# Sixth slab of filler products moved from the softmax heads to the recurrent heads, in both mixings of a two-block model

## The reference, cut to what matters

```python
def token_mixing(x, norm_g, w_in, ..., w_out):
    h = rmsnorm(x, norm_g)
    proj = h @ w_in            # pool, ml q k v o i f, fox q k v f, and 3 x 1024 gate columns
    ...
    y_pool = pool_mixer(u_pool, pool_w_grp, pool_scale) @ w_br_pool
    y_ml = mlstm_mixer(ml_q, ml_k, ml_v, ml_o, ml_i + ml_b_i, ml_f + ml_b_f, ml_norm_g) @ w_br_ml
    y_fox = fox_mixer(fx_q, fx_k, fx_v, fx_f + fox_b_f) @ w_br_fox
    gts = jax.nn.sigmoid(gate_pre).reshape(gate_pre.shape[:-1] + (N_BRANCH, D_MODEL))
    merged = gts[..., 0, :] * y_pool + gts[..., 1, :] * y_ml + gts[..., 2, :] * y_fox
    return merged @ w_out
```

## Time and profile before

| what | value |
|---|---|
| median of 3 runs | 2291.81 us (2286.31 to 2295.19) |
| profiled execution, its own time | 2291.82 us |
| its span, first to last instruction | 2290.1 us |
| TensorE matmul busy | 2216.6 us, 97% |
| TensorE weight load busy | 1579.4 us, 69% |
| VectorE busy | 883.7 us, 39% |
| ScalarE busy | 393.3 us, 17% |
| mean granted TensorE clock | 0.985 |

### The profile page before, as it was taken

How to read it: one execution, slowest core, us unless ns; L and a number is a source line. 1 busy time by engine, 2 the same in 40 slices (tenths; PEclk the granted TensorE clock), 3 DMA queues, 4 the chain that set the end, 5 groups by cost and what they waited for, 6 DMA issues and landing times. The chain is left out here.

```text
span 2290.1 us, 49032 instructions
## 1 busy us (share of the span) xinstructions
PE 2216.6 (97%) x22096; PEld 1579.4 (69%) x22096; DVE 883.7 (39%) x1657; ACT 393.3 (17%) x822; POOL 169.4 (7%) x250
## 2 busy tenths in 40 slices
PE   8999999999999999999999999999998999899998
PEld 7699889998689973535353534344446877689997
DVE  2676455452566431010000100111013374768764
ACT  0242311100233320000000010000001342224302
POOL 1000100000000012000000000000001162400000
PEclk9999999999999999999999999999999997899999
DMA  7423354434333377999999999999997211055440
GB/s 248 148 93 130 122 210 158 162 129 166 111 108 123 102 276 281 403 387 393 416 411 417 413 411 414 409 415 408 415 404 261 94 38 39 10 189 187 148 182 20
DMA packets 170559, 540.96 MB, mean 236 GB/s; under 512 B 17068, under 2 KB 35022, under 8 KB 153966
## 3 DMA queue, kind: packets, MB, share of 16 engines
q1 hardware_dynamic: 154144, 528.81, 60.0%
q10 hardware_dynamic: 14622, 4.16, 0.8%
q0 software_dynamic: 1584, 4.85, 0.5%
HBM read 532.94 MB, written 4.85 MB: 235 GB/s over the span
## 5 line engine op out<-in xcount | busy, mean ns | idle before, releaser
L183 PE MATMUL bank<-ring,moe_he 128*32 128x512 f32 (+2 forms) x6144 | 577.7, 537 | 2.8 <-DMA ring<-in_moe_w_up 2.7
L183 PEld LDWEIGHTS bank<-ring,moe_he 128*32 128x32 f32 x6144 | 198.7, 110 | 376.6 <-issue 367.7
L183 PE MATMUL bank<-hT,ring 128*128 128x128 f32 (+1 forms) x1952 | 290.7, 307 | 9.7 <-PEq L932 3.4
L183 PE MATMUL bank<-ring,moe_actT 128*32 128x256 f32 x5352 | 292.3, 379 | 1.3 <-DMA ring<-in_moe_w_down 1.3
L183 PEld LDWEIGHTS bank<-hT,ring 128*128 128x128 f32 x1952 | 263.4, 191 | 33.4 <-issue 8.8
L183 PEld LDWEIGHTS bank<-ring,moe_actT 128*32 128x32 f32 x5352 | 174.1, 110 | 116.9 <-issue 3.9
L2784 DVE TENSOR_TENSOR moe_act<-moe_silu,bank 128x512 f32<-128x512 f32 (+2 forms) x48 | 26.8, 614 | 540.4 <-PE bank L183 540.4
L183 PE MATMUL bank<-ring 128*128 128x128 f32 (+2 forms) x976 | 121.8, 284 | 1.4 <-ACT ring L826 1.4
L183 PEld LDWEIGHTS bank<-ring 128*128 128x128 f32 (+1 forms) x976 | 115.8, 190 | 4.0 <-ACT ring L826 1.8
L183 PE MATMUL bank<-kept,ring 128*128 128x256 f32 (+1 forms) x448 | 96.6, 378 | 6.1 <-PEq L1709 3.0
L183 PEld LDWEIGHTS bank<-kept,ring 128*128 128x128 f32 x448 | 83.2, 198 | 18.5 <-issue 5.4
(11 more groups left out here) (841 smaller groups left out, 2553.1 us busy)
## 6 DMA issues: line engine op xcount, KB each, us to landing
ring<-in_moe_w_down SPq DMA_DIRECT2D x55, 2048.0 KB, 19.1
ring<-in_moe_w_gate SPq DMA_DIRECT2D x32, 2048.0 KB, 23.2
ring<-in_moe_w_up SPq DMA_DIRECT2D x32, 2048.0 KB, 22.8
ring<-in_w_in SPq DMA_DIRECT2D x29, 2048.0 KB, 8.0
ring<-in_moe_w_gate SPq DMA_DIRECT2D x28, 1536.0 KB, 18.1
ring<-in_moe_w_up SPq DMA_DIRECT2D x28, 1536.0 KB, 14.6
ring<-in_w_up SPq DMA_DIRECT2D x10, 2048.0 KB, 11.9
ring<-in_w_out SPq DMA_DIRECT2D x6, 2048.0 KB, 7.9
```

The costliest lines, as they stand in the source:

```text
L183: ins = pe.matmul(out, lhsT, rhs, start=start, stop=stop, **kw)
```

## The change

The unit list of the recurrent block gets a sixth slab (42 units in place of 35), the list of the softmax block loses it (30 in place of 37). The counts are set anew, and VectorE's sums and additions stand at other places of its stream.

```diff
-MIX_LATER = 5
-MLSTM_SHARES = (2,) * 16 + (3,)
+MIX_LATER = 6
+MLSTM_SHARES = (2, 3) + (3, 2, 3, 2) * 3 + (2, 2, 3)
 FOX_LEAD = 2
 FOX_FIRST = (3,) * 8
-FOX_SECOND = (2, 2, 2, 1, 1, 1, 1, 1)
+FOX_SECOND = (1, 1, 0, 1, 0, 1, 0, 0)
@@ fox_units
-    return branch(0) + seven(5) + branch(1) + seven(6) + branch(2) + seven(7) + branch(3)
+    return branch(0) + seven(6) + branch(1) + seven(7) + branch(2) + branch(3)
@@ mlstm, VectorE, head i
                 divide(i)
                 if 2 <= i + 1 < ML_HEADS:
                     weigh(i + 1)
-                if i < 2:
-                    fill.add_00(v, k, i)
+                if i == 0:
+                    fill.add_00(v, k, 0)
                 elif i == 2:
-                    fill.add_rest(v, k, 2)
-                else:
-                    fill.add_rest(v, k, 3)
-                    fill.sum_weights(v, k, 4)
-                norm(i)
-                if i < 2:
-                    fill.add_rest(v, k, i)
-                    fill.sum_weights(v, k, i + 1)
-                    exponents(i + 2)
-                if i == 1:
-                    fill.add_00(v, k, 2)
-                elif i == 2:
-                    fill.sum_weights(v, k, 3)
                     fill.add_00(v, k, 3)
                 elif i == 3:
                     fill.add_00(v, k, 4)
                     fill.add_rest(v, k, 4)
+                    fill.sum_weights(v, k, 5)
+                norm(i)
+                if i == 0:
+                    fill.add_rest(v, k, 0)
+                if i < 2:
+                    fill.sum_weights(v, k, i + 1)
+                    if i == 1:
+                        fill.add_00(v, k, 2)
+                    exponents(i + 2)
+                if i == 0:
+                    fill.add_00(v, k, 1)
+                    fill.add_rest(v, k, 1)
+                elif i == 1:
+                    fill.add_rest(v, k, 2)
+                    fill.sum_weights(v, k, 3)
+                elif i == 2:
+                    fill.add_rest(v, k, 3)
+                    fill.sum_weights(v, k, 4)
+                elif i == 3:
+                    fill.add_00(v, k, 5)
+                    fill.add_rest(v, k, 5)
@@ attention, VectorE, behind the copy of head i's transposes
-                    if i in (0, 2, 4):
-                        if i == 4:
-                            fill.add_rest(v, k, 6)
-                        fill.sum_weights(v, k, 5 + i // 2)
-                    elif i in (1, 3, 5):
-                        fill.add_00(v, k, 5 + i // 2)
-                    if i in (1, 6):
-                        fill.add_rest(v, k, 5 if i == 1 else 7)
+                    if i == 0:
+                        fill.sum_weights(v, k, 6)
+                    elif i in (1, 4):
+                        fill.add_00(v, k, 6 if i == 1 else 7)
+                    elif i in (2, 5):
+                        fill.add_rest(v, k, 6 if i == 2 else 7)
+                        if i == 2:
+                            fill.sum_weights(v, k, 7)
```

## The result

The changed kernel takes 2327.44 us in the median of 4 runs (2325.86 to 2328.39), the kernel before 2292.21 beside it: ratio 1.0151, 95% interval 1.0138 to 1.0165. It is 35.2 us slower. The forecast was 28 us slower, at 2320 with a range to 2331. The profiled execution has a span of 2325.9 us, 35.8 more than before.

The account below looks back on a forecast made before the run. TensorE was taken to bound both blocks. Per mixing 12.5 + 9.9 - 2.95 - 7.0 + 1.7 = 14.1 us, for two mixings 28.2, on a median of 2291.81 gives 2320 us, range 2311 to 2331.

Parts of the forecast that it names:

- The three waits: Recurrent block: new TensorE waits at product 13 (head 0, 2.8 us), 21 (head 1, 6.2) and 34 (head 2, 0.9).
- 0.17: TensorE in general: a displayed wait is 0.17 us shorter than what it costs.
- 12.5 + 9.9 - 2.95: Recurrent block, us per mixing: seven added products 12.5, new waits 9.9, old waits removed 2.95.
- The half microsecond of cover: Recurrent head 2: the square is ready about 0.5 us before TensorE reaches it; if missing, up to 1 us more.
- Softmax block: Softmax block, us per mixing: 10.8 saved, 2.7 and 1.1 lost to waits, net -7.0.
- The waits on the copy of the transposes: Softmax heads 2, 4, 6 and 7: no product covers VectorE's copy, 0.9 us each; head 7's lies under the tail.
- the one in head 1: Softmax head 1: a product waits for ScalarE's copy of the next product behind its exponentials, 1.1 us lost.
- the last unit: Softmax head 7: the last filler after the transposes was free under VectorE's tail, so its 1.73 us is not saved.
- the clock's term: Recurrent head 1: the 6.2 us wait lowers TensorE's clock once in each mixing, 1.7 us lost.
- more clock loss: Rival: head 0's wait trips the clock too, 2323, or head 1's cold stretch is longer, 2329; chance 0.25.
- No clock loss: Rival: both blocks' waits come as worked out but the clock stays up, 2317; chance 0.15.
- the sum of slab 2 would be met earlier: Rival: in the recurrent block make4 of slab 2 and additions come earlier than read, 2297 or 2289; chance 0.08.

Follow-up runs that it names:

- the first experiment: The changed kernel with the weight sums that begin with make4 of slab 2 placed ahead of head 1's norm, not behind it; 2306.45 us, ratio 1.0065.
- the second experiment: The changed kernel with slab 2's weight sums ahead of head 1's norm and additions of slabs 0 and 3 ahead of their heads' norms; 2303.9 us, ratio 1.0047.
- the last kernel: The changed kernel with all sums and additions of slabs 0 to 3 ahead of the norms and softmax units dealt out anew; 2283.42 us, ratio 0.9956.
- the third: The changed kernel with 24 idle matmuls on TensorE behind head 1's mean square; 2321.77 us, ratio 1.012.
- the five-slab kernel with sooner sums: The kernel before, five slabs in the recurrent block, with additions and sums placed sooner there; 2286.45 us, ratio 0.9972.
- the softmax experiment: The changed kernel with the softmax block's 30 units dealt out otherwise, one behind every head's transposes; 2317.16 us, ratio 1.0113.
- the five-slab kernel with the new tail: The five-slab kernel with sooner sums, with two of head 7's three first units put behind its transposes; 2283.4 us, ratio 0.9956.

## Why the prediction was right, and where it fell short

**Direction and mechanism: right.** The measured 2327.4 lies in the upper part of the range, 7 us above the forecast. The forecast was that moving products can win only the waits of the earlier trace rows and would make three new ones. All three came, at the products named, and taking their causes away took them away.

**The three waits: right to a tenth.** Forecast 2.8, 6.2 and 0.9; measured 2.75 (6.65 less 3.90), 6.17 (6.61 less 0.44) and 0.87 (0.70 displayed and 0.17). Without the clock the recurrent block of the first mixing grew by 24.0 - 2.84 - 1.78 = 19.4, where 12.5 + 9.9 - 2.95 is 19.45. The half microsecond of cover in front of head 2's mean square held.

**Softmax block: right within half a microsecond.** Forecast -7.0, measured -6.65 and -6.6. The waits on the copy of the transposes cost 0.87 each, and the one in head 1 0.95 displayed, 1.12 in full. The tail from the transposes to the merge is as long as before (287.07 to 293.48 is 6.41, and so is 270.36 to 276.77), so the last unit was free, as said. Of the four waits at the transposes three lie on the path. What is missing, 0.4, fits a part of a wait's price that was left out: behind each of these three and the one in head 1 the next piece starts 0.1 us later than they do without one (the output matmuls at 280.80 and 281.33 are 0.53 apart, those of the kernel before at 272.09 and 272.52 only 0.43), four times. In the recurrent block three waits went and three came, so it cancels there.

**The step that failed is the clock's term.** It stood in the sum as one loss of 1.7 us in each mixing. Measured:
- behind head 1's wait 2.84 and 2.61, since the stretch at 1.2 GHz lasted over 5 us and not the some 3.4 that cost 1.7 in the earlier trace rows;
- behind head 0's wait 1.78 in the first mixing (the two wide products take 5.24 us from 136.31 to 141.55, not 3.46) and nothing in the second. This was the rival "more clock loss", and it came by half; the wait was 2.60 displayed, to be set beside the 2.79 of the earlier trace rows, and not the 2.8 that had the 0.17 in it;
- in front of the merge 1.7 in each mixing, which was in no term and no rival. I had priced the last unit behind head 7's transposes at nothing because the block's end did not move. But it had kept TensorE's idle time ahead of the merge at 2.1 us, which is 2.9 without it, and in this kernel the slow merge followed in both mixings. That the longer idle time is the cause is likely and not shown: the first experiment had it as well, and its merges were quick.

That is 6.3 and 4.3 us where the sum had 1.7 and 1.7, 7.2 more. With the 0.8 of the two softmax blocks, 28.2 becomes 36.2, and the blocks show 36.1. That the total comes out as well owes something to luck: behind the first merge the kernel before lost 1.45 us at a product where the changed one didn't (16 records took 6.73 us at 531.60 and 5.28 at 550.00, both behind 3.05 idle), and other such differences go the other way.

**The rivals.** No clock loss is refuted by the rows at 0.50. That the sum of slab 2 would be met earlier is refuted by the 6.0 us wait; what it would have been worth is shown by the second experiment, with the sum and the additions early and the softmax block as changed: 2303.9, above the rival's 2297 by the slow merges and product 14's wait in the main, and still slower than the kernel before. Only with the softmax block dealt out anew as well, in the last kernel, was the time on the other side.

**The rule beside it.** The Trainium skill's rule that every long idle gap is charged on its own (TensorE: Matmul & The Clock Gate, HAM oscillation - how this bites in real kernels) agrees in that the places were charged each on its own: three in the first mixing here, two in the second, where my sum had one. Which gaps are long enough it doesn't settle for this kernel, since those of 2.6 and 2.9 us were charged in some profiles and not in others.

## What to carry to other kernels

Work moved into a block that already hides its filler is worth only the waits that go; before moving it, write out which product then stands behind which step of each other engine's stream, and put every sum or addition that doesn't depend on a head's chain ahead of the wait for that chain. Idle time of TensorE has a second price when its clock falls: a filler that doesn't move the end of a block may still shorten the idle time ahead of the next one. If a wait can't be avoided, idle matmuls in it can give the second price back, as they did in head 1 (2.8 and 2.5 us); but look at the blocks behind as well, since ahead of the first merge the gain was lost again in the next block. When a reordering loses, take its two halves apart: here sooner sums and additions were a gain for the old split, and the new split was neutral once its own stood ahead of the norms.

## What the runs showed of the hardware that I had not expected

The clock's fall is not a fixed function of the idle time at these lengths. The same idle 2.9 to 3.0 us ahead of the merge was followed by a slow merge in both mixings of the changed kernel, in both of the second experiment, in one of the two of the third, and in neither of the first:

```profile
283.80 14.05 PE L183 MATMUL bank<-fq,ring 128*128 128x256 f32 x64 [2.90 <-PEq L1271]
```

That row is of the first experiment, with the same idle time and the same matmuls as the 15.74 above. An idle 2.1 us gave one slow merge in the five-slab kernel with sooner sums (15.74) and none in the kernel before, and head 0's 2.6 us was followed by slow products in the first mixing of four kernels out of five and in no second mixing. At the entry of the second mixing's local mixers, 2.8 us idle was followed by a slow start in all ten profiles. What decides between them was not tried. For the reader it means that profiles can differ by 1.7 us at a place where their kernels are the same. It adds up: the stretch from the second mixing's routing matmul (884.58 in the changed kernel) to the product at 1995.25, the same in all ten kernels, took 1102.9 to 1111.8 us. The two shortest are those of the softmax experiment and of the repaired six-slab kernel, whose profiled executions lie 3.5 and 4.9 us below their medians. Comparisons of a few microseconds want the medians for the total, and the blocks' own lengths for the cause.

The other is VectorE beside POOL. One addition of 128x512 floats took 0.69 us on VectorE when POOL was not at work and 1.63 when POOL's had started first. In the rows seen it matters which of the two starts first. These are the first gated multiplications of both engines in the five-slab kernel with the new tail, in the first and in the second mixing:

```profile
264.79 1.27 POOL L1435 TENSOR_TENSOR merged<-merged,gate_logits_a 128x512 f32<-128x512 f32 x1 [158.14 <-ACT gate_logits_a L1424]
264.81 1.80 DVE L1435 TENSOR_TENSOR merged<-merged,gate_logits_a 128x512 f32<-128x512 f32 x1 [1.91 <-ACT gate_logits_a L1424]
...
785.23 0.69 DVE L1435 TENSOR_TENSOR merged<-merged,gate_logits_a 128x512 f32<-128x512 f32 x1 [1.91 <-ACT gate_logits_a L1424]
785.27 1.78 POOL L1435 TENSOR_TENSOR merged<-merged,gate_logits_a 128x512 f32<-128x512 f32 x1 [81.10 <-ACT gate_logits_a L1424]
```

The one that starts later, by 0.02 and by 0.04 us, is the one that is long. In the first pair VectorE's step ends 0.55 us behind POOL's, and so it does in the two rows of the softmax experiment above (287.33 and 286.78), as if it ran only once POOL's had ended. VectorE's three steps take 1.80, 1.64 and 1.64 us in the first mixing and 0.69, 1.16 and 1.64 in the second, and the block is 0.9 us longer in the first, as it is in all three kernels whose softmax block was dealt out anew. This was seen in the rows and not tried by itself.
